# HGRN2 decay-level scores in 64 x 64 blocks on the two halves of the output partitions, in a fused hybrid-decoder step on one core

## Chip, cores, metric

One NeuronCore of a Trainium2 chip. The metric is the device time of one launch in microseconds, lower is better. The kernel before runs in 2715.94 us (median of three runs, 2710.35 to 2718.6).

## What is computed

The reference is one inference step of a two-layer decoder trunk (`D_MODEL` 2048, 512 prompt tokens and 8 single-token samples, all float32). Each layer projects the normalised input to the columns of 16 heads of width 128 (4 HGRN2, 6 mLSTM, 6 retention), runs the recurrences, gates the result and projects it back. The change is in the HGRN2 heads:

```python
b = jnp.cumsum(gc, axis=2)                       # gc: log forget gate, per key channel
diff = b[:, :, :, None, :] - b[:, :, None, :, :]
decay = jnp.exp(jnp.where(mask[:, :, None], diff, -jnp.inf))
a = jnp.einsum('bhtk,bhsk,bhtsk->bhts', qc, kc, decay)
intra = jnp.einsum('bhts,bhsv->bhtv', a, vc)
```

The score of query t and key s is a sum over 128 channels, each with its own decay from s to t, so one matmul of q and k doesn't give it.

## The kernel before

Tokens stand along the free axis: 512 prompt tokens and 8 samples, 520 columns, in two halves of 260 (`HALF`). Every weight tile of 2048 x 128 is multiplied by the normalised input in a split of three products: `quarter` (L501 to L512) issues, for each of 16 row blocks, high weights by high input, high weights by low input and low weights by high input, twice each for the two halves (all of them are recorded as L509). `tile` (L605 to L613) runs a tile as 8 parts of 12 matmuls. Each head has four tiles (for HGRN2: forget gate, query, value, output gate). TensorE (PE) executes in program order. The small matmuls of a head are "hooks" that stand between the parts of later tiles, so that the waits of the recurrence lie beside projection work.

An HGRN2 head works on four chunks of 128 tokens. The score matrix `a` (a view of buffer `t1`: partitions are keys s, four chunks, 128 queries t) is built level by level. Level -1 is the diagonal (key and query of the same token, `k` times `x1`). Level v = 0 to 6 holds the pairs whose tokens lie in one group of 2^(v+1), the key in its first half and the query in its second. For it, the keys are decayed to the end of their half (`kdec(v)`, made by `k_step(v)` on VectorE (DVE) as one multiply and one copy of 256 elements a partition, L1338 and L1339) and the queries from the start of theirs (`q_step(v)`, in place in `qd`, L1344).

`level_scores` (L701 to L722) is the hook. For a level it waits for the queries (`vs["lev"]`), from level 3 on also for its PSUM bank to be free again (`vs["pred"]`), and multiplies, for each of four chunks, 128 keys by 128 queries into partitions 0 to 127 of bank `(lv + 1) % 4` of `mx` (L716 for level -1, L719 for the others). Levels -1 and 0 stand together after part 2 of the head's value tile, levels 1 to 5 after parts 3 to 7, level 6 after part 0 of the output-gate tile (L794 to L796). Then `rows` follows after part 2 (transposes, L515 and L518), `states_u` after part 5 (L733, L737), `outputs` after part 7 (L745, L747, L756) and `back` after part 5 of the next head's first tile.

DVE, in its own program order, makes the key levels 1 to 4 together with the products of decays `fold(m)` (L1355 to L1359), then the level-0 queries (L1362), and then for each level (L1365 to L1378): wait for the score, make the next level's queries, signal them, and take the score out of PSUM. The diagonal is taken by a multiply with the identity, which writes zeros elsewhere (L1372); each other level by a predicated copy of 128 x 512 with the level's mask (L1374). After levels 1, 2 and 3 it makes key levels 5, 6 and 7. `kdec(7)` is used only by `rows` (L671).

Other queues: ScalarE (ACT) takes projections out of PSUM and makes the high part of the weights, GpSimd (POOL) the low part (L480), SP issues the weight loads. Matmuls in which the output has few partitions are placed at partitions 0, 32, 64, 96 in several parts of the kernel: the adaLN projection (L590 and L575, 32 weight columns), the gates (L629, 6 columns), the sample rows (L518, 2 columns, and L756).

Of the kernel before, what the change touches and what calls it, by code (L numbers as in the profile page):

```python
# [126 lines left out]
def program(nc, x_prompt, x_sample, st_hg, st_c, st_n, st_m, st_conv, st_rt, c_prompt, c_sample, g_norm,  # L127
# [3 lines left out]
    with ExitStack() as ctx:  # L131
# [137 lines left out]
        def kdec(m):  # L269

            return k[:, 0:T] if m == 0 else lev[:, m - 1, :]
# [228 lines left out]
        def _(e):  # L500
# [47 lines left out]
            for l in range(DEPTH):  # L548
# [102 lines left out]
                def hooks_of(h):  # L651
# [49 lines left out]
                        def level_scores(vs_range):  # L701

                            def run():
                                for lv in vs_range:
                                    if lv < 0:
                                        e.wait_ge(as_["kk"], n + 1)
                                        e.wait_ge(taken, ht(g, 1))
                                    else:
                                        e.wait_ge(vs["lev"], n * LEVELS + (lv + 1))
                                    if lv >= 3:  # L710
                                        e.wait_ge(vs["pred"], n * (LEVELS + 1) + (lv - 2))
                                    bank = (lv + 1) % 4
                                    for c in range(NC):
                                        cs = slice(c * CH, (c + 1) * CH)
                                        if lv < 0:
                                            last = e.matmul(mx[:, bank, cs], k[:, cs], x1[:, PAD + c * CH:PAD + (c + 1) * CH],  # L716
                                                            start=True, stop=True)
                                        else:
                                            last = e.matmul(mx[:, bank, cs], kdec(lv)[:, cs], qd[:, cs],  # L719
                                                            start=True, stop=True)  # L720
                                    last.then_inc(ps["score"], 1)
                            return run  # L722

# [363 lines left out]
        def _(e):  # L1087
# [53 lines left out]
            for l in range(DEPTH):  # L1141
# [100 lines left out]
                for h in range(NH):  # L1242
# [39 lines left out]
                        if kind == "rt":  # L1282
                            chunk_decay, token_decay = hc[:, HC_CD:HC_CD + NC], hc[:, HC_G:HC_G + NS]
                            e.wait_ge(hc_in[g % 2], 16 * (n // 2 + 1))
                            e.wait_ge(rope_in, 16 * (l + 1))
                            rope(0, q)
                            tt(qd[:], q[:, 0:T], hc[:, HC_IN:HC_IN + T], M)
                            rope(1, k)
                            e.drain().then_inc(vs["qk"], 1)

                            e.wait_ge(ps["score"], scorec(l, kind, i, 1))
                            tt(a, mx[:, 0, :].rearrange("p (c t) -> p c t", c=NC), bc(hc[:, HC_D:HC_D + CH], 1, NC),
                               M)
                            e.drain().then_inc(vs["a"], 1)
                        elif kind == "ml":
                            chunk_decay, token_decay = gcol[:, i, 3, :], gsb[:, i, :]
                            e.wait_ge(ps["bcast"], n + 1)
                            tt(dt[:].rearrange("p (c t) -> p c t", c=NC), mx[:, 0, :].rearrange("p (c t) -> p c t", c=NC),
                               bc(gcol[:, i, 0, :], 2, CH), A_)
                            e.drain()  # L1300
                            tt(dt[:].rearrange("p (c t) -> p c t", c=NC), dt[:].rearrange("p (c t) -> p c t", c=NC),
                               bc(cst[:, C_NEG:C_NEG + 128], 1, NC), A_)
                            e.drain().then_inc(vs["r"], 1)
                            e.wait_ge(taken, ht(g, 0))
                            e.wait_ge(as_["cvc"], n + 1)
                            conv(0, t1, "conv_q")
                            e.wait_ge(as_["lg"], 2 * n + 1)
                            log_sigmoid(t3[:], t1[:], "ls")
                            e.wait_ge(as_["silu"], 2 * n + 1)
                            tt(q[:], t1[:], t3[:], M)  # L1310
                            e.wait_ge(taken, ht(g, 1))
                            conv(1, t2, "conv_k")
                            e.wait_ge(as_["iw"], n + 1)
                            tt(qd[:], q[:, 0:T], iw, M)
                            e.drain().then_inc(vs["qd"], 1)
                            e.wait_ge(as_["lg"], 2 * n + 2)
                            log_sigmoid(t4[:], t2[:], "ls")
                            e.wait_ge(as_["silu"], 2 * n + 2)
                            stt(k[:], t2[:], SCALE, t4[:], M, M)
                            e.drain().then_inc(vs["qk"], 1)  # L1320
                            e.wait_ge(ps["score"], scorec(l, kind, i, 1))
                            tt(t1[:, 0:T], mx[:, 0, :], dt[:], M)
                            e.drain().then_inc(vs["a"], 1)
                        else:
                            chunk_decay, token_decay = sm[:, 16:16 + NC], t3[:, T:TOK]

                            def paired(ap, m):

                                return ap.rearrange("p (n s x) -> p n s x", s=2, x=1 << (m - 1))

                            def folded(m, s):

                                return fold(m - 1)[:, s::2].unsqueeze(2).broadcast_to([P, T >> m, 1 << (m - 1)])

                            def k_step(m):

                                new, old = paired(kdec(m), m), paired(kdec(m - 1), m)
                                tt(new[:, :, 0, :], old[:, :, 0, :], folded(m, 1), M)  # L1338
                                e.tensor_copy(new[:, :, 1, :], old[:, :, 1, :])  # L1339

                            def q_step(m):

                                w = paired(qd[:], m)
                                tt(w[:, :, 1, :], w[:, :, 1, :], folded(m, 0), M)  # L1344

                            e.wait_ge(as_["l1"], n + 1)
                            f = x0[:, PAD:PAD + TOK]
                            stt(t2[:], f, 0.0, t1[:], MIN, S_)
                            e.drain()
                            tt(t4[:], t2[:], f, S_)  # L1350
                            e.drain().then_inc(vs["d1"], 1)
                            e.wait_ge(as_["kk"], n + 1)
                            ts(t3[:], t3[:], lbv[:, 1, i:i + 1], lbv[:, 0, i:i + 1], M, A_)
                            e.drain()
                            for m in range(1, LEVELS + 1):  # L1355
                                tt(fold(m), fold(m - 1)[:, 0::2], fold(m - 1)[:, 1::2], M)
                                if m <= 4:
                                    k_step(m)
                                e.drain()  # L1359

                            e.wait_ge(taken, ht(g, 1))
                            tt(qd[:], x1[:, PAD:PAD + T], t3[:, 0:T], M)  # L1362
                            e.drain().then_inc(vs["lev"], 1)
                            e.sem_inc(vs["qk"], 1)
                            for lv in range(LEVELS):  # L1365
                                e.wait_ge(ps["score"], scorec(l, kind, i, lv + 2))
                                q_step(lv + 1)
                                e.drain().then_inc(vs["lev"] if lv + 1 < LEVELS else vs["kw"], 1)
                                for x in (-1, 0) if lv == 0 else (lv,):
                                    bank = mx[:, (x + 1) % 4, :].rearrange("p (c t) -> p c t", c=NC)  # L1370
                                    if x < 0:
                                        tt(a, bank, bc(ident, 1, NC), M)  # L1372
                                    else:
                                        e.copy_predicated(a, bc(lmask[:, 128 * x:128 * x + 128], 1, NC), bank)  # L1374
                                    e.drain().then_inc(vs["pred"], 1)
                                if 1 <= lv <= 3:
                                    k_step(lv + 4)
                                    e.drain()  # L1378
                            e.sem_inc(vs["a"], 1)


# [176 lines left out]
```

## Time and profile before

| | us |
|---|---|
| median of 3 runs | 2715.94 (2710.35 to 2718.6) |
| the profiled execution | 2717.08 |
| its span, first to last instruction | 2715.3 |
| PE busy with matmuls | 2492.0 (92%) |
| DVE busy | 1142.8 (42%) |
| POOL busy | 932.8 (34%) |
| ACT busy | 795.9 (29%) |

A record is one instruction in the trace. A float32 matmul leaves two MATMUL records and two weight-load records (a transpose leaves one of each), so `level_scores` leaves 8 records of each kind for a level. The ends of matmuls are modelled and include the way through the array, so of a run of matmuls the distance of starts counts, not the duration. In the timeline, a row "x8" with a start and a length merges eight records; their mean distance is the length less the duration of one, divided by seven. The HGRN2 heads of the first layer lie at 264 to 510 us of the span, those of the second at 1527 to 1772 us.

### The profile page before, as it was taken

The page shows a single profiled execution, that of the slowest core. Times are in us where ns is not written, and L with a number is a line of the kernel's source. Part 1 is how long each engine was busy: PE and PEld are TensorE (multiplying, and loading weights), DVE is VectorE, ACT ScalarE, POOL GpSimd, SP SyncE. Part 2 cuts the span into 40 slices and gives each one's busy share as a digit, 9 for nine tenths or more (in the row PEclk, how much of TensorE's full clock was granted, in tenths as well). Part 3 has the DMA queues.
Part 4 walks back from the last instruction along what each step waited for, and adds up shares of the span by engine and source line. Part 5 has one row for each costly group of instructions (what it writes and reads, how often), then busy time and mean ns, then how long its engine had stood idle before and what let it go on. Part 6 is the DMA issues. An engine that isn't in the chain of part 4 may idle for free.

```text
span 2715.3 us, 48497 instructions
## 1 busy us (share of the span) xinstructions
PE 2492.0 (92%) x20592; PEld 2244.4 (83%) x20592; DVE 1142.8 (42%) x2239; ACT 795.9 (29%) x1247; POOL 932.8 (34%) x676
## 2 busy tenths in 40 slices
PE   3776999799999999989998799979999999998996
PEld 2115999699999999987776799969999999998995
DVE  2004555367767433430000755546677534333002
ACT  1004222233433332331112322323333323333113
POOL 0002343233434444462221343414434444446440
PEclk9998999899999999999999899989999999998998
DMA  5995333133334343429987233323333333433421
GB/s 176 319 310 156 90 85 96 49 83 100 96 96 103 103 113 101 108 67 299 294 277 236 70 81 93 80 68 87 94 104 100 103 105 101 110 97 95 116 80 63
DMA packets 473218, 339.70 MB, mean 125 GB/s; under 512 B 17701, under 2 KB 416513, under 8 KB 471681
## 3 DMA queue, kind: packets, MB, share of 16 engines
q1 hardware_dynamic: 473002, 336.61, 43.1%
q8 instruction: 162, 2.65, 0.4%
q14 instruction: 54, 0.44, 0.1%
HBM read 304.72 MB, written 32.04 MB: 124 GB/s over the span
## 4 chain that ended last, share of the span: by engine, by line
PE 76%; DVE 8%; DMA 7%; ACT 3%; DVEq 2%; POOL 2%; issue 1%; SPq 1%; ACTq 0%
PE pj L509 59%; DMA raw<-in_w_ada 4%; PE mx L515 2%; PE mx L544 2%; PE mx L719 2%; DMA raw<-in_w_out 2%; POOL wlo L480 1%; PE pj L590 1%; ACT whi L862 1%; PE mx L575 1%; PE mx L518 1%; DVE t L1095 1%; PE mx L733 1%; PE mx L629 1%; DVEq L1188 1%
## 5 line engine op out<-in xcount | busy, mean ns | idle before, releaser
L480 POOL TENSOR_TENSOR wlo<-raw,whi 128x512 fp32r<-128x512 f32 x640 | 890.3, 1422 | 1710.6 <-ACT whi L862 1710.6
L509 PE MATMUL pj<-hh,whi 128*128 128x260 f32 x5120 | 1067.6, 290 | 61.9 <-POOL wlo L480 33.2
L509 PE MATMUL pj<-hh,wlo 128*128 128x260 f32 x5120 | 1036.7, 284 | 0.0
L509 PE MATMUL pj<-hl,whi 128*128 128x260 f32 x5120 | 1035.6, 284 | 0.0
L509 PEld LDWEIGHTS pj<-hh,whi 128*128 128x128 f32 x5120 | 793.5, 190 | 139.9 <-issue 101.6
L509 PEld LDWEIGHTS pj<-hl,whi 128*128 128x128 f32 x5120 | 795.5, 190 | 0.0
L509 PEld LDWEIGHTS pj<-hh,wlo 128*128 128x128 f32 x5120 | 795.0, 190 | 0.0
L862 ACT ACTIVATE whi<-raw 128x2048 fp32r<-128x2048 f32 x160 | 306.3, 1915 | 314.5 <-DMA raw<-in_w_out 170.7
L1095 DVE SCALAR_TENSOR_TENSOR o<-pj,mod,t 128x260 f32<-128x260 f32 x64 | 28.0, 480 | 397.8 <-PE pj L509 397.8
L862 ACT ACTIVATE xv<-pj 128x260 f32<-128x260 f32 x192 | 66.2, 384 | 433.7 <-PE pj L509 433.3
L590 PE MATMUL pj<-raw,sct 128*32 128x512 f32 x384 | 102.5, 668 | 45.9 <-DMA raw<-in_w_ada 45.4
L862 ACT ACTIVATE t<-t 128x520 f32<-128x520 f32 (+1 forms) x132 | 84.3, 639 | 186.1 <-DVEq L1279 133.3
L590 PEld LDWEIGHTS pj<-raw,sct 128*32 128x32 f32 x384 | 14.5, 113 | 124.5 <-DMA raw<-in_w_ada 122.9
L1095 DVE SCALAR_TENSOR_TENSOR t<-xv,prm,t 128x512 f32<-128x512 f32 x96 | 103.6, 1099 | 5.5
L862 ACT ACTIVATE z<-pj 128x260 f32<-128x260 f32 x64 | 21.3, 385 | 271.4 <-PE pj L509 271.4
L862 ACT ACTIVATE t<-pj 64x260 f32<-64x260 f32 (+1 forms) x108 | 43.8, 405 | 152.2 <-PE pj L590 151.1
L1089 DVE TENSOR_TENSOR mod<-mx,bia 128x432 f32<-128x432 f32 x2 | 1.2, 607 | 174.8 <-PE mx L561 173.7
L1089 DVE TENSOR_TENSOR xv<-xv,lev 128x520 f32<-128x520 f32 x24 | 16.8, 701 | 136.0 <-ACT t L862 135.5
L862 ACT ACTIVATE zw<-zw 128x520 f32<-128x520 f32 x96 | 61.3, 638 | 24.2 <-DVEq L1252 19.9
L1409 DVE COPY st<-mx 128x128 f32<-128x128 f32 (+1 forms) x32 | 9.4, 293 | 131.2 <-PE mx L737 131.2
L1089 DVE TENSOR_TENSOR t<-mx,hc 128x512 f32<-128x512 f32 x12 | 8.3, 693 | 130.1 <-PE mx L697 130.1
L515 PE MATMUL mx<-cst,xv 128*128 128x128 f32 (+1 forms) x376 | 54.2, 275 | 3.9 <-DVEq L1484 3.7
(231 smaller groups left out, 2229.3 us busy)
## 6 DMA issues: line engine op xcount, KB each, us to landing
raw<-in_w_in SPq DMA_DIRECT2D x256, 512.0 KB, 5.3
raw<-in_w_ada SPq DMA_DIRECT2D x96, 512.0 KB, 5.4
raw<-in_w_out SPq DMA_DIRECT2D x64, 512.0 KB, 6.2
lev<-in_w_ada SPq DMA_DIRECT2D x58, 512.0 KB, 4.9
xv<-in_w_ada SPq DMA_DIRECT2D x38, 512.0 KB, 5.5
out<-ss SPq DMA_DIRECT2D x32, 512.0 KB
y_kept<-o SPq DMA_DIRECT2D x2, 4160.0 KB, 12.8
t<-y_kept SPq DMA_DIRECT2D x32, 260.0 KB, 4.5
```

What stands on the lines that cost most here:

```text
L480: last = e.tensor_tensor(wlo[:, par, cs], w[:, cs], whi[:, par, cs].bitcast(F32), ALU.subtract)
L509: last = e.matmul(pj[:, 2 * par + b, 0:HALF], w[:, par, kb * P:(kb + 1) * P], x[:, kb, b * HALF:(b + 1) * HALF], start=(kb == 0 and m == 0 ...
L515: return e.transpose(out, src, cst[0:n, C_ID:C_ID + n])
L518: return e.matmul(out, src, cst[0:n, C_ID:C_ID + n], start=True, stop=True)
L544: last = e.matmul(mx[:, b, 0:HALF], ones, (t1, t2)[kb % 2][:, b * HALF:(b + 1) * HALF], start=(kb == 0), stop=(kb == KB - 1))
L575: last = e.matmul(mx[r:r + 32, n % 2, :], sct[:, kb, :], ada_slot(piece)[:, j, :], start=(kb < 4), stop=(kb >= KB - 4))
L590: last = e.matmul(pj[r:r + 32, n % 2, :], sct[:, kb, :], raw[:, s % RAW, j * ADA_N:(j + 1) * ADA_N], start=(kb < 4), stop=(kb >= KB - 4))
L629: last = e.matmul(mx[32 * j:32 * j + H_ML, 0, 0:HALF], w, x[:, kb, (j // 2) * HALF:(j // 2 + 1) * HALF].bitcast(F32), start=(kb == 0 and m ...
L719: last = e.matmul(mx[:, bank, cs], kdec(lv)[:, cs], qd[:, cs], start=True, stop=True)
L733: last = e.matmul(mx[:, c, 0:w], kt[:, c, :], vt[:, c, 0:w], start=True, stop=True)
L862: return e.activation(out, in_, func, **kw)
L1095: return e.scalar_tensor_tensor(out=out, in0=a_, scalar=s, in1=b_, op0=op0, op1=op1)
```

## The change

In the scores, the chunk's 128 keys and 128 queries are cut into blocks of 64. Levels -1 to 5 have pairs only inside the two diagonal blocks, so two matmuls of 64 weight columns by 64 moving columns are issued for a chunk: block b goes to output partitions 64b to 64b+63, and the bank then holds 256 columns instead of 512. Level 6 has pairs only between the first 64 keys and the second 64 queries: one matmul a chunk, into partitions 0 to 63.

```diff
 for c in range(NC):
-    cs = slice(c * CH, (c + 1) * CH)
-    if lv < 0:
-        last = e.matmul(mx[:, bank, cs], k[:, cs], x1[:, PAD + c * CH:PAD + (c + 1) * CH],
-                        start=True, stop=True)
-    else:
-        last = e.matmul(mx[:, bank, cs], kdec(lv)[:, cs], qd[:, cs],
-                        start=True, stop=True)
+    for b in range(1 if lv + 1 == LEVELS else 2):
+        s0 = c * CH + 64 * b
+        t0_ = s0 + 64 if lv + 1 == LEVELS else s0
+        key = k if lv < 0 else kdec(lv)
+        query = x1[:, PAD + t0_:PAD + t0_ + 64] if lv < 0 else qd[:, t0_:t0_ + 64]
+        last = e.matmul(mx[64 * b:64 * b + 64, bank, 64 * c:64 * c + 64],
+                        key[:, s0:s0 + 64], query, start=True, stop=True)
 last.then_inc(ps["score"], 1)
```

On DVE the lower left quarter of `a`, which no selection writes any more, is zeroed once per head; key levels 5 to 7 are made before the levels; each selection becomes two instructions, one for each half of the partitions, of 64 partitions by 256 elements; level 6 is a plain copy.

```diff
+e.memset(a[64:128, :, 0:64], 0.0)
 e.wait_ge(taken, ht(g, 1))
 tt(qd[:], x1[:, PAD:PAD + T], t3[:, 0:T], M)
 e.drain().then_inc(vs["lev"], 1)
 e.sem_inc(vs["qk"], 1)
+for m in range(5, LEVELS + 1):
+    k_step(m)
+    e.drain()
 for lv in range(LEVELS):
     e.wait_ge(ps["score"], scorec(l, kind, i, lv + 2))
     q_step(lv + 1)
     e.drain().then_inc(vs["lev"] if lv + 1 < LEVELS else vs["kw"], 1)
     for x in (-1, 0) if lv == 0 else (lv,):
-        bank = mx[:, (x + 1) % 4, :].rearrange("p (c t) -> p c t", c=NC)
-        if x < 0:
-            tt(a, bank, bc(ident, 1, NC), M)
-        else:
-            e.copy_predicated(a, bc(lmask[:, 128 * x:128 * x + 128], 1, NC), bank)
+        bank = mx[:, (x + 1) % 4, 0:256].rearrange("p (c t) -> p c t", c=NC)
+        for b in range(1 if x + 1 == LEVELS else 2):
+            r = slice(64 * b, 64 * b + 64)
+            if x < 0:
+                tt(a[r, :, r], bank[r], bc(ident[r, r], 1, NC), M)
+            elif x + 1 == LEVELS:
+                e.tensor_copy(a[0:64, :, 64:128], bank[r])
+            else:
+                mk = lmask[r, 128 * x + 64 * b:128 * x + 64 * b + 64]
+                e.copy_predicated(a[r, :, r], bc(mk, 1, NC), bank[r])
         e.drain().then_inc(vs["pred"], 1)
-    if 1 <= lv <= 3:
-        k_step(lv + 4)
-        e.drain()
```

## Rows read from the trace of the kernel before

**Rows 1.** The page: busy time of the engines, chain that ended last.

```profile
PE 2492.0 (92%) x20592; PEld 2244.4 (83%) x20592; DVE 1142.8 (42%) x2239; ACT 795.9 (29%) x1247; POOL 932.8 (34%) x676
...
PE 76%; DVE 8%; DMA 7%; ACT 3%; DVEq 2%; POOL 2%; issue 1%; SPq 1%; ACTq 0%
```

**Rows 2.** 264 to 510 us: PE, PEld, DVE, ACT, POOL busy; clock, DMA. PE's waits.

```profile
264.00:510.00 246.00, 242.61 (x2110) 234.93 (x2114) 129.06 (x302) 70.45 (x106) 92.40 (x64) 1.00 0.33 86
...
PE mx L515 <- DVEq L1484: 2.9, 4, 0.8
```

**Rows 3.** The chain in order of time, first head: start, length, what.

```profile
282.04 0.89 PE mx L716 x8
...
283.82 1.44 PE pj L509 x12
285.26 0.89 PE mx L719 x8
```

**Rows 4.** PE timeline, single levels and the projection matmuls behind them.

```profile
282.77 1.06 PE L719 MATMUL mx<-qd,xv 128*128 128x128 f32 x8
...
283.90 0.40 PE L509 MATMUL pj<-hl,whi 128*128 128x260 f32 x2
...
74.90 1.06 PE L561 MATMUL mx<-cst,t 128*128 128x9 f32 x8
```

**Rows 5.** Weight loads by shape: busy us, mean ns.

```profile
L719 PEld LDWEIGHTS mx<-qd,lev 128*128 128x128 f32 x384 | 46.9, 191 | 0.0
...
L575 PEld LDWEIGHTS mx<-lev,sct 128*32 128x32 f32 x232 | 6.0, 108 | 5.9 <-DMA lev<-in_w_ada 2.0
```

**Rows 6.** Timeline of matmuls and weight loads placed at several output partitions.

```profile
73.92 0.62 PE L590 MATMUL pj<-raw,sct 128*32 128x512 f32 x2 [0.94 <-DMA raw<-in_w_ada]
...
73.92 1.05 PE L590 MATMUL pj<-raw,sct 128*32 128x512 f32 x4 [0.94 <-DMA raw<-in_w_ada]
...
73.92 0.14 PEld L590 LDWEIGHTS pj<-raw,sct 128*32 128x32 f32 x4 [1.85 <-DMA raw<-in_w_ada]
...
509.84 0.62 PE L629 MATMUL mx<-hh,gw 128*6 128x260 f32 x8
510.28 0.62 PE L629 MATMUL mx<-hl,gw 128*6 128x260 f32 x8
```

**Rows 7.** Timeline around the sample rows and around an 11-column transpose.

```profile
301.26 0.27 PE L515 MATMUL mx<-cst,lev 128*128 128x128 f32 x1
301.46 0.29 PE L518 MATMUL mx<-cst,xv 128*2 128x128 f32 x4
...
301.79 0.51 PE L518 MATMUL mx<-cst,xv 128*2 128x128 f32 x12
...
302.57 0.28 PE L509 MATMUL pj<-hl,whi 128*128 128x260 f32 x1
...
560.47 0.38 PE L515 MATMUL mx<-cst,xv 128*11 128x128 f32 x2
560.60 0.49 PE L509 MATMUL pj<-hh,whi 128*128 128x260 f32 x2
```

**Rows 8.** DVE timeline of the first head's levels; a zero fill (busy, mean ns).

```profile
279.90 0.69 DVE L1089 TENSOR_TENSOR qd<-xv,t 128x512 f32<-128x512 f32 x1
283.86 0.61 DVE L1089 TENSOR_TENSOR qd<-qd,t 128x256 f32<-128x256 f32 x1 [3.27 <-PE mx L719]
...
285.40 0.74 DVE L1374 COPY_PREDICATED t<-lmask,mx 128x512 f32<-128x512 uint8 x1
286.26 0.43 DVE L1089 TENSOR_TENSOR qd<-qd,dt 128x256 f32<-128x256 f32 x1
...
287.66 0.43 DVE L1089 TENSOR_TENSOR lev<-lev,dt 128x256 f32<-128x256 f32 x1
288.00 0.29 DVE L1339 COPY lev<-lev 128x256 f32<-128x256 f32 x1
...
L1118 DVE MEMSET nr<- 128x256 f32 x1 | 0.3, 272 | 0.0
```

## The prediction

> **What bounds the kernel now.** I read the page first: PE is busy for 92% of the span and makes 76% of the chain that ended last, while DVE is busy for 42% [rows 1]. The change touches only the eight HGRN2 heads (four in each layer), so the stretch counts, not the average. Over the first layer's four heads (246 us), PE is busy for 242.61 us and DVE for 129.06, at a granted clock of 1.00, the upper level of 2.4 GHz. The one repeated wait of PE there is 2.9 us in four, before the transposes of `back`, and none stands before a level's score [rows 2]. The chain in order of time runs through PE there: a level takes 0.89 us, the 12 matmul records of the projection part behind it take 1.44 us, then comes the next level [rows 3]. So PE's program is the bound in these stretches. What a hook gains or loses on PE reaches the end, and what DVE does costs nothing while it is ready before PE's next level.
>
> **What a level costs PE now.** Eight records, (1.06 - 0.27) / 7 = 0.11 us apart [rows 4], make the 0.89 us. The adaLN sums of L561 have the same weight load of 128 columns and only 9 moving columns, and stand (1.06 - 0.26) / 7 = 0.11 us apart too [rows 4]: the load of 128 columns takes that time by itself, and the stream of 128 columns about the same, beside it.
>
> **What 64 by 64 records cost.** The load shrinks with the weight columns: a mean of 191 ns for 128 and 108 for 32 is 0.86 ns a column [rows 5], or 0.055 us for 64. The stream: the gates start four records of 260 columns, one for each quarter of the output partitions, every 0.22 us (eight in 510.28 - 509.84 = 0.44 us) [rows 6], 0.85 ns a column, so 0.054 us for 64. With 3 to 5 ns between records, as 0.111 is above 128 times 0.85, I take 0.058 us.
>
> Do the two halves run together? Nothing here is placed in two halves, but much in quarters. In the adaLN projection two matmuls of different quarters both start at 73.92, and all four are done after 1.05 us, two times 0.43 and the way through the array; the four weight loads lie within 0.14 us, before the first two streams end [rows 6]. So for parts of different output partitions both loads and streams overlap, and I take the same for halves. A level of 16 records is then eight pairs, 8 x 0.058 = 0.46 us. Level 6 has eight records all in the lower half, which take turns, and costs 8 x 0.058 = 0.46 us as well.
>
> **What the change adds on PE: two switches a hook.** Where a matmul of all output partitions is followed by one placed in a part, the distance isn't 0.11 but 301.46 - 301.26 = 0.20 us, so going in costs 0.09. The last of the sample rows starts at 301.79 + 0.51 - 0.27 = 302.03; the second pair of projection matmuls behind it starts at 302.57, 0.54 later [rows 7]. Behind a level of before that distance is 283.90 - (282.77 + 1.06 - 0.27) = 0.34 [rows 4]. Going out costs 0.20. The first load of 64 columns lies bare behind the switch, 0.055. Together 0.345, say 0.35 us for each hook, paid seven times a head.
>
> **The sum on PE**
> - Hook with levels -1 and 0: before 16 x 0.111 = 1.78 us. After 2 x 0.46 + 0.35 = 1.27. Gain 0.51.
> - Five hooks with levels 1 to 5: before 0.89, after 0.46 + 0.35 = 0.81. Gain 0.08 each, 0.40.
> - Hook with level 6: the same, 0.08.
> - A head gains 0.99 us, eight heads 7.9 us.
>
> The bounds of the two terms that no row shows for halves: the distance of pairs lies between 0.055 (half of 0.11) and 0.065 us (if a few ns more go to each record), the switch between 0.29 (the bare load hidden) and 0.40. The best corner gives 0.61 + 6 x 0.16 = 1.57 us a head, 12.6 in all; the worst 0.34 + 6 x -0.03 = 0.16 us a head, 1.3 in all.
>
> **DVE, beside PE.** Added before the level-0 queries: a zero fill of 256 elements, at most 0.27 us. Moved ahead: three key steps, each of a multiply (287.66) and a copy that ends at 288.29, with its drain 0.74 us, so 2.2. Together 2.5 us go into the 3.27 us in which DVE waited for the first score [rows 8]. That score now comes 0.7 us earlier (0.93 + 0.145 for the way in, against 1.78), so the idle time left is about 0.1 us; and the level-1 scores stand 1.44 us later in PE's program, against 0.61 for the queries. Each selection in two instructions costs a little more than in one: 256 elements take 0.43 against 0.69 for 512, and the second can start 0.34 us after the first (as 288.00 follows 287.66), so 0.77 against 0.69, and alike for the predicated copies. Two levels' selections take some 0.16 more, and the level-2 queries, signalled at 286.70 before [rows 8] with PE coming for them at about 287.3 (level 1 of rows 3 and 0.89 + 1.44, less 0.16 by which the chain counts later than the timeline, less a load of 0.11), are signalled at about 286.3 with PE coming at 287.3 - 0.51 - 0.08 = 286.7. All later levels are rid of a key step of 0.74 and the cadence of PE's levels (2.24 us) is longer than DVE's work for one (about 1.5). So DVE costs nothing, as long as halves of 64 partitions cost by their elements a partition. If that cover of 0.4 us goes, PE waits for level 2. The step is moved past no DMA and no other queue; `rows` gets `kdec(7)` earlier than it needs.
>
> **Rivals**
> - **The halves take turns.** Then 16 records cost 16 x 0.058 = 0.93 us: levels 1 to 5 lose 0.93 + 0.35 - 0.89 = 0.39 each, the double hook 1.86 + 0.35 - 1.78 = 0.43, level 6 gains 0.08. A head loses 2.3 us, eight lose 18.4: 2734 us. It decides once less than 0.7 of the overlap is had (all of it is worth 7 x 0.46 = 3.2 us a head, of which 2.3 are needed to be even). For it: no row shows halves. Against it: all placed matmuls of rows 6 and 7 overlap.
> - **Loads don't run beside a stream.** Then a pair takes 0.055 + 0.054, 0.11 us, a level 0.89 as before, and each hook the 0.35 of its switches more than now: 7 x 0.35 x 8 = 19.6 us, 2736. Against it: the four loads in 0.14 us, beside streams of 0.43 [rows 6]. The Trainium skill, "TensorE: Matmul & The Clock Gate", section "The mechanism" of the part on packing small matmuls, says this: a weight load overlaps matmuls in flight only when its row group differs, and here all row groups are the same. The trace disagrees with it.
> - **DVE comes late.** Were a selection of 64 partitions as long as one of 128 (0.69 and 0.74 each), the level-2 queries would come 2 x 0.55 later than I have them, about 0.7 us after PE wants them, and the later ones would catch up. Eight times 0.7 gives back 5.6: 2713.6 us.
> - **No separate placement.** The 11-column transposes are followed by projection 0.13 us after their start, without a switch [rows 7]. If the 64-column matmuls were treated so, 16 records in turn would cost 0.93 without switches: 7 x 0.04 lost, 0.43 gained at level 6, 0.15 a head: 2715 us. Against it: the upper half must go to partitions 64 to 127.
>
> **How the numbers follow.** The profiled execution took 2717.08 us (span 2715.3), 1.1 above the median of 2715.94. I take the 7.9 from the median: 2708 us. The same step from the profiled execution gives 2709.2. Measurements of this kernel tell a difference of about 0.3%, 8.1 us, from none, and the forecast lies at that edge. Chances: forecast 0.66 (2703 to 2715), DVE late 0.12, no placement 0.06, halves in turn 0.12, loads in series 0.04. Of the forecast's 0.66 I give 0.40 to over 0.3% faster and 0.26 to within; DVE late and no placement fall within 0.3%; the last two are slower. That makes 0.40, 0.44, 0.16. The range is 2702 to 2720: it takes in the corners and leaves out the two slower cases and a tail below.
>
> **What would show it.** Per level 16 score records of 64 columns in pairs some 5 to 10 ns apart, pairs 0.058 us apart; in the chain 0.8 us from part to part instead of 0.89, and the double hook 1.27 instead of 1.78; the distance of two heads' `rows` shorter by 1.0 us. Right on DVE: no wait of PE for `qd`, and DVE's first wait for a score under 0.5 us. The prediction is wrong if records of the upper half start only after those of the lower, if the step from the last score to the second pair of projection matmuls is longer than 0.54 less 0.05, or if PE waits for DVE at level 1 or 2.

## The result, and the profile after

The changed kernel runs in 2734.92 us (median of four runs), the kernel before in 2715.04 in the same comparison: a ratio of 1.0071, 95% interval 1.0056 to 1.0086. It is slower by 20 us, where 8 us faster was forecast. The profiled execution has a span of 2733.7 us against 2715.3.

The page shows that PE's work didn't grow: its busy time is what it was [rows 1], while its share of the chain fell from 76% to 70%.

```profile
PE 2493.2 (91%) x21040; PEld 2233.1 (82%) x21040; DVE 1184.9 (43%) x2303; ACT 796.4 (29%) x1247; POOL 937.6 (34%) x676
...
PE 70%; DVE 11%; DMA 6%; ACT 5%; DVEq 3%; issue 2%; POOL 1%; ACTq 1%; SPq 0%
```

The view of PE's waits over the whole span has a row that no view of before had. L1372 is the drain behind the level queries, the instruction with which DVE waits for its own multiply to end before it signals, so PE stands 24.1 us before scores and waits for queries, up to 3.2 us at a time:

```profile
PE mx L719 <- DVEq L1372: 24.1, 10, 3.2
```

The PE timeline of the first head shows both halves of the story (start, length, group; in brackets the idle time before it). Levels -1 and 0 are exactly what was forecast; the wait stands before level 1:

```profile
280.01 0.41 PE L509 MATMUL pj<-hh,wlo 128*128 128x260 f32 x2
280.35 0.69 PE L719 MATMUL mx<-xv 128*64 128x64 f32 x16
280.86 0.64 PE L719 MATMUL mx<-qd,xv 128*64 128x64 f32 x16
281.43 0.51 PE L509 MATMUL pj<-hh,whi 128*128 128x260 f32 x2
281.77 0.41 PE L509 MATMUL pj<-hl,whi 128*128 128x260 f32 x2
...
286.00 0.69 PE L719 MATMUL mx<-qd,lev 128*64 128x64 f32 x16 [2.87 <-DVEq L1372]
```

The weight loads of the first 16 records lie beside their matmuls:

```profile
280.35 0.55 PEld L719 LDWEIGHTS mx<-xv 128*64 128x64 f32 x16
```

The chain from the wait, in order of time, shows that the wait costs more than its own length:

```profile
286.00 0.69 PE mx L719 x16
286.69 2.51 PE pj L509 x12
289.20 1.05 PE mx L719 x16
290.25 1.76 PE pj L509 x12
292.01 0.61 PE mx L719 x16
292.63 1.63 PE pj L509 x12
```

The same part of 12 records takes 2.51 us behind the wait and 1.63 later (the switches included), the level 1.05 instead of 0.61. The windows view of the two stretches (PE, PEld, DVE, ACT, POOL busy, then the granted clock) gives the reason: the granted clock is 0.62 behind the wait and 1.00 after it, part of the stretch at the lower of the two levels, 1.2 GHz.

```profile
286.00:290.50 4.50, 4.50 (x45) 4.08 (x46) 3.24 (x8) 0.00 (x0) 0.00 (x0) 0.62 0.84 225
290.50:300.00 9.50, 9.50 (x110) 8.69 (x110) 5.70 (x13) 2.47 (x3) 0.91 (x1) 1.00 0.01 2
```

The last two columns, the share of the DMA engines and GB/s, show a burst of transfers in the same stretch. It isn't the cause: behind the wait of the second head, also of 2.9 us, the DMA share is as high, the clock stays at 1.00, and the parts take 1.62 us as usual:

```profile
350.10:354.60 4.50, 4.25 (x55) 3.90 (x56) 3.87 (x9) 0.00 (x0) 0.00 (x0) 1.00 0.81 221
```

So the clock falls behind most of these waits, not behind all: behind six of the eight in this execution, by the granted clock of the 4.5 us after each (0.62 to 0.65, else 1.00).

Why the queries are late is in DVE's timeline of the same head, with POOL's row under it:

```profile
278.61 0.69 DVE L1089 TENSOR_TENSOR qd<-xv,t 128x512 f32<-128x512 f32 x1
279.51 1.22 DVE L1089 TENSOR_TENSOR lev<-lev,dt 128x256 f32<-128x256 f32 x1 [0.21 <-issue]
280.65 1.36 DVE L1339 COPY lev<-lev 128x256 f32<-128x256 f32 x1
282.09 1.36 DVE L1089 TENSOR_TENSOR lev<-lev,dt 128x256 f32<-128x256 f32 x1
283.37 1.35 DVE L1339 COPY lev<-lev 128x256 f32<-128x256 f32 x1
284.79 0.43 DVE L1089 TENSOR_TENSOR lev<-lev,dt 128x256 f32<-128x256 f32 x1
285.13 0.28 DVE L1339 COPY lev<-lev 128x256 f32<-128x256 f32 x1
285.49 0.42 DVE L1089 TENSOR_TENSOR qd<-qd,t 128x256 f32<-128x256 f32 x1
...
278.67 5.90 POOL L480 TENSOR_TENSOR wlo<-raw,whi 128x512 fp32r<-128x512 f32 x4 [5.57 <-ACT whi L862]
```

The key steps are the instructions of [rows 8], moved to the time from 279.5 on. There POOL works at the low part of a weight tile, from 278.67 to 284.57. Four of the six take 1.22 to 1.36 us instead of 0.43 and 0.29; the pair behind POOL's end takes its old time. The three steps last 5.9 us, not 2.2, and the level-1 queries are signalled at 285.9, where PE wanted them at about 283.1. Both layers' heads do the same.

Where the time went can be measured by stage: from the first level score of a layer's first head to the first matmul of the gates (L629), a stretch with four heads in it, 227.96 and 226.87 us before, 239.41 and 239.81 after. Both layers together give 454.8 and 479.2 us, so 24.4 us more. The spans differ by 18.4; the missing 6 lie mostly in layer one's output stage and the start of layer two, with 5.2 of them between the gates of layer one and the first score of layer two. The change doesn't touch that stretch, and in the runs below it varies between 1028 and 1037 us, so the stage sums are the sharper measure for all of them.

### The profile page after: what moved, and what is told of

Same layout as the page of the kernel before. It is cut to its first block, busy times and chain, and to the rows that moved or that the text cites. A ratio compares the mean times of both kernels' runs of the same rounds, so it can differ in the third digit from the quotient of the medians.

```text
span 2733.7 us, 49457 instructions
## 1 busy us (share of the span) xinstructions
PE 2493.2 (91%) x21040; PEld 2233.1 (82%) x21040; DVE 1184.9 (43%) x2303; ACT 796.4 (29%) x1247; POOL 937.6 (34%) x676
## 4 chain that ended last, share of the span: by engine, by line
PE 70%; DVE 11%; DMA 6%; ACT 5%; DVEq 3%; issue 2%; POOL 1%; ACTq 1%; SPq 0%
PE pj L509 54%; DMA raw<-in_w_ada 4%; PE mx L515 2%; ACT whi L862 2%; PE mx L544 2%; DVE lev L1089 1%; PE mx L575 1%; DVE t L1095 1%; POOL wlo L480 1%; PE pj L590 1%; ACT t L862 1%; PE mx L719 1%; PE mx L518 1%; PE mx L733 1%; PE mx L629 1%
```

## The experiments

Theory A: the PE saving is as forecast, and the loss comes from the key steps ahead of the levels, because there they run beside POOL. Theory B: the blocks or the selections in halves make PE late. All ratios are to the kernel before on the same chip, with 95% intervals. "Stage" is the sum defined above, "waits" are PE's at the level scores.

| run | ratio | stage, us | waits, us |
|---|---|---|---|
| before | | 454.8 | none |
| the change | 1.0071 (1.0056 to 1.0086) | 479.2 | 24.1 in 10 |
| e1 keys back | 0.9955 (0.9941 to 0.9969) | 445.8 | none |
| e2 before, keys ahead | 1.0085 (1.0065 to 1.0106) | 480.8 | 16.1 in 8 |
| e3 POOL light | 0.9946 (0.9925 to 0.9968) | 445.8 | none |
| e4 keys spread | 0.9948 (0.9927 to 0.9969) | 445.8 | none |
| e5 halves in turn | 1.0025 (1.0010 to 1.0039) | 463.3 | none |
| e6 level 6 in pairs | 0.9953 (0.9926 to 0.9979) | 444.3 | none |
| e7 two steps ahead | 1.0057 (1.0040 to 1.0073) | 470.3 | 19.2 in 13 |
| e8 one step ahead | 0.9981 (0.9972 to 0.9990) | 453.4 | 6.4 in 16 |
| e9 POOL cut in 8 | 1.0072 (1.0045 to 1.0098) | 486.4 | 21.1 in 8 |
| e10 before, POOL light | 1.0008 (0.9992 to 1.0025) | 454.8 | none |
| e11 as e6, more rounds | 0.9956 (0.9942 to 0.9970) | 444.3 | none |
| e12 e6 and POOL cut in 8 | 0.9937 (0.9923 to 0.9951) | 442.7 | none |

### Undo the move: e1 and e4

```diff
-for m in range(5, LEVELS + 1):
-    k_step(m)
-    e.drain()
 for lv in range(LEVELS):
     ...
+    if 1 <= lv <= 3:          # e4: if lv in (1, 3, 5): k_step(5 + lv // 2)
+        k_step(lv + 4)
+        e.drain()
```

> The change, but key levels 5 to 7 made behind levels 1 to 3 again, as before. Theory A (the key steps ahead of the levels run beside GpSimd's low parts, are stretched from some 2.2 us to 5.9 us by them, and make PE wait 2.9 us for the level-1 queries in each head): PE's waits for L719 fall from 24.1 us to under 2 us, no clock window at half level inside the heads, and the PE saving stands: 2707 to 2710 us. DVE's work for levels 1 to 3 is then 0.55 + 1.0 + 0.85 = 2.4 us against PE's 2.24, so up to 0.1 us of wait a head at level 4 or 5. Theory B (selections in halves or the blocks themselves make PE late): stays above 2725 us.

> The change, but key level 5 made behind level 1, 6 behind 3, 7 behind 5. Theory A: DVE's work for two levels is 1.55 + 2.4 = 3.95 us against PE's 4.48, so PE never waits for L719: 2707 to 2709 us, as e1 or up to 1 us below it. Theory B: above 2725 us.

Both came out as theory A has them, a little faster than their bands (by 1.0 and 0.3 us): 2705.96 and 2706.73 us, no wait at the scores, and a stage sum of 445.8 us, 9.0 less than before. The heads follow each other every 59.63 us in e4, against 60.61 in layer two of before: 0.98 us a head, for 0.99 forecast. Theory B falls. The PE timeline of e4 has the cadence of the forecast, 284.32 - 282.08 = 2.24 us a level:

```profile
282.08 0.69 PE L719 MATMUL mx<-qd,lev 128*64 128x64 f32 x16
282.69 0.51 PE L509 MATMUL pj<-hh,whi 128*128 128x260 f32 x2
283.04 0.40 PE L509 MATMUL pj<-hl,whi 128*128 128x260 f32 x2
...
284.32 0.69 PE L719 MATMUL mx<-qd,lev 128*64 128x64 f32 x16
```

### The move alone: e2

```diff
 e.sem_inc(vs["qk"], 1)
+for m in range(5, LEVELS + 1):
+    k_step(m)
+    e.drain()
 ...
-    if 1 <= lv <= 3:
-        k_step(lv + 4)
-        e.drain()
```

> The kernel before, with only one part of the change: key levels 5 to 7 ahead of the levels. Theory A: DVE is at them from 280.8 to about 286.5 us in the first head, the level-1 queries come near 287 where PE wants them at 285.0: about 2 us of wait in each of eight heads, 16 us, and some falls of the clock of 0.9 us each: 2731 to 2737 us. Theory B, or if the steps fit into DVE's 3.27 us of waiting: 2714 to 2718 us.

The waits are as theory A has them, 2.0 us in each of eight heads, and the steps are stretched alike (1.22, 1.36, 1.34 and 1.36 us for the first four). The time is 2742.44 us, 5 above the expected band: the stage grew by 26 us, of which 16.1 are waits and 10 what came behind them, so I had that part too low.

```profile
PE mx L719 <- DVEq L1371: 16.1, 8, 2.0
```

### Take POOL away: e3, and its control e10

```diff
-    low(i * 4 + (l * TILES + j), j % 2)
+    low(i * 4 + (l * TILES + j), j % 2, 16 if i < H_HG and j == 3 else None)
```

`low` then makes 16 columns in each of its four instructions for these tiles and leaves out the other 496, so these weights lack most of their low part.

> The change as it is, but GpSimd makes only 16 of 512 columns of each quarter of the low part for the HGRN2 heads' output-gate tiles (the rest of that low part is left out), so that it is idle while DVE makes key levels 5 to 7. Theory A: each key multiply takes 0.42 and each copy 0.29 us again, DVE's first queries come about 283.2 us, PE's waits for L719 vanish: 2706 to 2710 us. Rival C (GpSimd has no part in it, the steps are slow there or simply too much): the steps stay at 1.2 to 1.36 us and the time at 2730 us or more.

> Control for the run with a light GpSimd: the kernel before, with the same part of the low weights left out (16 of 512 columns in the HGRN2 heads' output-gate tiles). Nothing waited for them, so 2712 to 2717 us, at most 3 us from the kernel before; if it gains 8 us or more, the light run of the change didn't show what theory A says.

This settles the cause. With the change's order kept, the timeline of DVE and POOL's row read:

```profile
277.80 0.42 DVE L1089 TENSOR_TENSOR lev<-lev,dt 128x256 f32<-128x256 f32 x1 [0.21 <-issue]
278.14 0.31 DVE L1339 COPY lev<-lev 128x256 f32<-128x256 f32 x1
278.52 0.42 DVE L1089 TENSOR_TENSOR lev<-lev,dt 128x256 f32<-128x256 f32 x1
...
276.95 1.58 POOL L480 TENSOR_TENSOR wlo<-raw,whi 128x16 fp32r<-128x16 f32 x4 [5.57 <-ACT whi L862]
```

The steps are back at 0.42 and 0.29 us, the three of them end at 279.9, 2.1 us after they began, and no wait is left: 2702.91 us, some 3 us below the expected band, with a stage sum of 445.8 as in e1. POOL isn't wholly idle there: its four short instructions run until 278.53, and the multiply and the copy beside them take 0.42 and 0.31 us. So it isn't POOL's being busy by itself that holds DVE, but the length of its instructions, which e9 tries again. The same lighter POOL gave the kernel before nothing (2713.79 us, ratio 1.0008, stage 454.8), so it isn't POOL's work as such that costs, only DVE's key steps beside it. Rival C falls.

### The dose: e7 and e8

```diff
-for m in range(5, LEVELS + 1):
+for m in range(5, 7):         # e8: range(5, 6)
     k_step(m)
     e.drain()
 ...
+    if lv == 3:               # e8: levels 6 and 7 behind 2 and 4
+        k_step(7)
+        e.drain()
```

> The change with key levels 5 and 6 ahead and 7 behind level 3. Theory A (the wait grows by what DVE does ahead while GpSimd works): in the change the third key step already ran behind GpSimd's end at its own 0.7 us, so the level-1 queries come 0.7 us earlier and PE waits 2.2 us a head instead of 2.9; with fewer falls of the clock: 2720 to 2730 us. If any step ahead of the levels makes PE wait by its own length alone (0.7 us), then 2708 to 2713 us.

> The change with key level 5 alone ahead, 6 behind level 2, 7 behind level 4. Theory A: the one step, stretched to 2.6 us, ends near 282.1 us in the first head's time of the change, about when the first score is there; the level-1 queries, themselves beside GpSimd, come near 283.2, as PE does: 0 to 0.4 us of wait a head, 2705 to 2711 us.

The waits come down from 24.1 to 19.2 and 6.4 us, as theory A orders them. In e7 they are 2.4 us a head, where 2.2 was expected, and it took 2731.51 us, 1.5 above its band. In e8 they are 0.8 us a head, twice the most expected: the level-1 wait is 0.42 to 0.44 us in seven heads and 1.57 in one, and a second of 0.23 us or a little more stands before level 2. Its time, 2709.36 us, lies in its band. The level-1 wait comes from the query multiply itself, which now starts beside POOL; the DVE timeline of e8:

```profile
283.20 1.22 DVE L1089 TENSOR_TENSOR lev<-lev,dt 128x256 f32<-128x256 f32 x1 [0.21 <-issue]
284.35 1.36 DVE L1339 COPY lev<-lev 128x256 f32<-128x256 f32 x1
285.78 1.35 DVE L1089 TENSOR_TENSOR qd<-qd,t 128x256 f32<-128x256 f32 x1
```

### What the stretch is made of: e9

```diff
-LOW_CUT = 4
+LOW_CUT = 8
```

> The change as it is, with GpSimd's low part cut into 8 instructions of 256 columns a tile instead of 4 of 512, the same work. Theory F (a DVE instruction with SBUF operands on both sides gets its turn only when a GpSimd instruction ends: in the change's trace four key instructions in a row take 1.22 to 1.36 us and end 0.15 to 0.3 us behind the ends of four GpSimd instructions of 1.3 to 1.8 us): the key instructions take about 0.7 us, the six of them some 4 us instead of 5.9, PE waits 1 to 1.7 us a head instead of 2.9: 2714 to 2724 us. Rival G (the two engines share bandwidth, so what counts is how long they overlap): the waits stay near 24 us, 2730 us or more.

The price missed, the mechanism held. The DVE timeline of e9's second head:

```profile
351.80 1.21 DVE L1089 TENSOR_TENSOR qd<-xv,t 128x512 f32<-128x512 f32 x1
353.22 0.66 DVE L1089 TENSOR_TENSOR lev<-lev,dt 128x256 f32<-128x256 f32 x1 [0.21 <-issue]
353.81 0.81 DVE L1339 COPY lev<-lev 128x256 f32<-128x256 f32 x1
354.69 0.80 DVE L1089 TENSOR_TENSOR lev<-lev,dt 128x256 f32<-128x256 f32 x1
355.41 0.82 DVE L1339 COPY lev<-lev 128x256 f32<-128x256 f32 x1
...
357.90 0.79 DVE L1089 TENSOR_TENSOR qd<-qd,t 128x256 f32<-128x256 f32 x1
...
351.72 6.69 POOL L480 TENSOR_TENSOR wlo<-raw,whi 128x256 fp32r<-128x256 f32 x8 [4.98 <-ACT whi L862]
```

Each DVE instruction now takes 0.66 to 0.82 us, about one of POOL's shorter instructions (a mean of 0.83 us in this run). Multiply and copy cost the same, though alone they take 0.42 and 0.29. So neither bandwidth nor length of overlap sets the time; the two engines take turns, one instruction each. Eight POOL instructions catch eight DVE instructions where four had caught four: the 0.69 us multiply of `qd` took 1.21, the six key instructions and the level-1 query multiply followed. Up to the end of that multiply the change needs 7.3 us from the start of `qd`, e9 6.9. The wait fell only from 24.1 / 8 = 3.0 to 2.6 us a head, and the ratio not at all (1.0072). DVE leaves such a stretch only when POOL does, if it has instructions enough to be caught by all of it: the last caught one ends at 284.72 in the change, where POOL ends at 284.57, and at 358.69 in e9, where POOL ends at 358.41.

The stage sum even grew, by 7.2 us, though the waits fell by 3.0: in this execution (2745.89 us, the slowest of the four) the clock fell behind all eight waits and stayed low for longer. Levels 1 and 2 and the parts behind them take 7.3 us in the second head, by the chain, where 4.5 is usual. The windows behind that head's wait:

```profile
358.80:363.30 4.50, 4.50 (x38) 4.16 (x40) 3.04 (x7) 0.00 (x0) 0.00 (x0) 0.50 0.88 230
363.30:367.80 4.50, 4.50 (x49) 4.17 (x46) 2.23 (x6) 0.00 (x0) 0.00 (x0) 0.80 0.01 4
```

Against it stands a shorter end of the kernel: from the first matmul of the gates of layer two to the last instruction it is 938.3 us instead of the change's 944.1.

### Do the halves overlap whatever the order: e5

```diff
-for c in range(NC):
-    for b in range(1 if lv + 1 == LEVELS else 2):
+for b in range(1 if lv + 1 == LEVELS else 2):
+    for c in range(NC):
```

> As e4, but PE's program has all four lower blocks of a level first and then the four upper ones. If PE starts records in program order (theory D), the halves overlap only at the seam: a level of 16 records takes some 0.87 us instead of 0.46, seven levels a head, eight heads: +23 us against e4, 2727 to 2732 us; this is also what the rival 'halves take turns' would have cost. If PE's queue reaches the upper half past the waiting lower ones (theory E; within a pair the two passes already start as lower, upper, lower, upper though the program has them lower, lower, upper, upper), then as e4: 2704 to 2709 us.

Between both: 2721.62 us, and 61.81 us a head against 59.63, 0.31 us for each of the seven levels where 0.41 would be no overlap but at the seam. In PE's timeline of e5 the first record of level 0 (`qd,xv`, by the program the lower half) starts at 290.23, when level -1 (`xv`) has three records (by the program of the upper half) left to start, and then the two alternate; a level by itself is the last row:

```profile
289.82 0.63 PE L719 MATMUL mx<-xv 128*64 128x64 f32 x11
290.23 0.27 PE L719 MATMUL mx<-qd,xv 128*64 128x64 f32 x1
290.28 0.22 PE L719 MATMUL mx<-xv 128*64 128x64 f32 x1
290.34 0.22 PE L719 MATMUL mx<-qd,xv 128*64 128x64 f32 x1
...
292.75 0.97 PE L719 MATMUL mx<-qd,lev 128*64 128x64 f32 x16
```

PE reaches past waiting records of one half to those of the other, but only a few deep (three in these rows). That PE executes in program order, as the section on the kernel before has it, therefore doesn't hold between the two halves. A level takes 0.97 us (to the modelled end) in blocks by halves and 0.69 alternating, so the alternation in the program is worth 15 us of this kernel.

### A version that beats both: e6, e11 and e12

Level 6 has eight records in one half. Its chunks 2 and 3 can go to the upper half, with DVE bringing them back:

```diff
-last = e.matmul(mx[64 * b:64 * b + 64, bank, 64 * c:64 * c + 64],
+up = c // 2 if lv + 1 == LEVELS else b
+last = e.matmul(mx[64 * up:64 * up + 64, bank, 64 * c:64 * c + 64],
 ...
-e.tensor_copy(a[0:64, :, 64:128], bank[r])
+e.tensor_copy(a[0:64, 0:2, 64:128], bank[0:64, 0:2])
+e.tensor_copy(a[0:64, 2:4, 64:128], bank[64:128, 2:4])
```

(with level 6's chunks in the order 0, 2, 1, 3, and the key steps as in e4).

> As e4, but level 6's blocks of chunks 2 and 3 go to the upper half of the partitions, so that its eight records run as four pairs too; DVE copies them back in two instructions of 64 x 128. Theory A: level 6 takes 0.23 us instead of 0.46: 1.8 us less over eight heads, 2703 to 2706 us; in the trace the hook's eight records start within 0.18 us. If DVE's two copies made PE late at the row transposes, there would be a wait at L515 behind DVE; none is expected, PE comes there 2.9 us later.

> The best version once more with more rounds (key steps spread behind levels 1, 3 and 5, level 6 in pairs): ratio to the kernel before 0.995 to 0.997, 2703 to 2708 us.

> The same with GpSimd's low part in 8 instructions. PE waits for nothing in the heads already, so no gain there: within 2 us of the run before it, unless GpSimd's longer total (a fixed cost for each instruction) shows where PE waits for it in the output stage, some 30 us in all now: then 2 to 5 us more.

The eight records of level 6 take 0.45 us to the modelled end in e11's PE timeline, not the 0.68 of e4:

```profile
297.32 0.45 PE L720 MATMUL mx<-qd,lev 128*64 128x64 f32 x8
```

That is 0.22 us a head (59.41 against 59.63), a stage sum of 444.3 us, and 2702.48 and 2702.10 us in two comparisons. The intervals of the ratios of e4, e6 and e11 overlap, so the gain over e4 rests on the stage sums and the head distances, not on the times. e12 adds the cut of POOL's work in 8 and is the fastest, 2697.74 us, ratio 0.9937, where I expected nothing or a small loss. Its stage sum is 442.7, 1.6 less than e11, with 59.23 us a head; I didn't trace which instructions bring the 0.18 us a head. The larger part of its gain lies outside the heads: from the first matmul of the gates of layer two to the end it takes 939.1 us, e11 943.7, as e9 did against the change. What makes that part shorter isn't traced either.

## Why the prediction was wrong, step by step

- **What bounds the kernel**: right. The stage sums in the table follow PE's own time, its waits and the clock behind them; e12's last 1.6 us are untraced.
- **Pairs overlap, 0.46 us a level**: right. In the change, pairs stand 0.058 us apart ((0.64 - 0.22) / 7 = 0.06 by the row at 280.86, for eight pairs). The rival of halves that take turns gives nearly the measured time, 2734 against 2734.92, and is wrong all the same: the two records of a pair start within 0.01 us, and with the key steps put back the same PE program gains 9 us. A time that fits is no proof of its mechanism.
- **Loads that don't run beside a stream**: refuted by the same rows: a pair every 0.058 us leaves no room for a load of 0.055 us in front of a stream of 0.054. The rule of the Trainium skill, "TensorE: Matmul & The Clock Gate", section "The mechanism", that a weight load overlaps matmuls in flight only when the row group differs, doesn't hold for the two column halves here.
- **Two switches, 0.35 us a hook**: right. From the last pair (280.86 + 0.64 - 0.22 = 281.28) to the second pair of projection matmuls at 281.77 it is 0.49 us, the 0.54 forecast from the sample rows less 0.05 of a shorter stream. The way in is 280.35 against the last projection matmul near 280.14, 0.21.
- **The sum on PE, 7.9 us**: right in mechanism and size once nothing stands in its way. The stage gained 9.0 us in e1 and e4, of which 8 x 0.98 = 7.8 is the forecast; the rest is in the main small waits of PE on DVE elsewhere in the heads: 4.7 us in both layers before, 2.9 of them in layer one [rows 2], and 3.6 in e4.
- **DVE, beside PE: the step that failed.** I put "2.5 us" into the "3.27 us in which DVE waited for the first score". The 2.5 came from key steps at 287.66, when POOL was idle; the gap they moved into is the one in which POOL works. Priced there, they take 5.9 us. [Rows 8] had the sign: the level-1 query multiply took 0.61 us and the next one, as large, 0.43. I read the gap for its length and not for who else was busy in it. What came is the last of the signs that the prediction names for its being wrong, a wait of PE for DVE at level 1. The rival "DVE comes late" had the right victim and a wrong cause (selections by halves, whose pairs cost 0.86 and 0.90 us, only some 0.1 more than forecast) and a price of 5.6 us for 24.1.
- **What a wait costs**: missing from the forecast altogether. The change's stage is 33.4 us above e4's and the waits make 24.1 of it. Most of the other 9.3 is the fall of the granted clock behind six of them: in the chain above, the two parts and the level between them take 5.32 us instead of 3.87, 1.45 more. Six times 1.45 is 8.7 us. Two of the six distances of heads in the change are 62.88 and 63.24 us, the other four 64.03 to 64.08; the two begin with the heads behind whose wait the clock stayed at 1.00, and they hold a second wait of 0.25 us that the four don't have. Why the clock fell behind some waits of the same length and not behind others stays open.

## To carry to other kernels

Before moving work into an engine's idle time, look at what the other engines do in that time and price the moved instructions by rows taken beside the same neighbour: in this kernel DVE's multiplies of two SBUF tensors and its copies within SBUF take turns with POOL's instructions, and DVE's reads of PSUM don't. Small matmuls in two halves of the output partitions run in pairs if the program alternates the halves, at 0.3 us or more of switches for each group, so such groups should be few and large. And a stall of PE of 2.9 us cost half as much again through the clock in six of eight cases.

## What the runs showed of the hardware

DVE beside POOL. The row of one form in the kernel before, both of its inputs in SBUF, has a median of 420 ns and a maximum of 1518 (min/median/max ns):

```profile
L1089 DVE TENSOR_TENSOR lev<-sr,cst x44: 406/420/1518, 302.9 to 2446.2; 98x256 f32<-98x256 f32 x44
```

The selections, which read scores from PSUM, are not caught. In the kernel before, the multiply with the identity at 284.59 lies whole beside POOL's last instruction (284.15 to 285.62) and takes the 0.69 us it takes alone; the predicated copies take 733 to 755 ns in all 56. Nor is every instruction that reads SBUF caught: the statistics of a head's output (BATCH_NORM_STATS2), with one input, take 274 to 297 ns in all 128, 80 of which lie beside POOL's work.

```profile
284.59 0.69 DVE L1089 TENSOR_TENSOR t<-mx,cst 128x512 f32<-128x512 f32 x1
...
L1460 DVE BATCH_NORM_STATS2 bst<-xv x128: 274/277/297, 318.5 to 2466.2; 128x6 f32<-128x128 f32 x128
```

POOL waits too: its four instructions of the first head take 5.90 us in the change and 5.33 before, where fewer DVE instructions meet them:

```profile
280.29 5.33 POOL L480 TENSOR_TENSOR wlo<-raw,whi 128x512 fp32r<-128x512 f32 x4 [5.55 <-ACT whi L862]
```

The Trainium skill, "GPSIMD Engine Reference", section "Specifications", names GpSimd's SBUF interfaces as shared with VectorE, with contention for DVE instructions in a two-port mode or with two SBUF inputs. The trace agrees in kind for the multiplies, and for the statistics, which have one input. The copies are caught as well; whether they run in a two-port mode, no run shows. The trace adds the size: each such DVE instruction takes about as long as the POOL instruction it meets, 1.36 us for 512 columns (the change) and 0.8 for 256 (e9).

PE places. The two records of a pair start together, and a switch between matmuls of all output partitions and placed ones costs 0.09 us in and 0.20 out. The Trainium skill, "TensorEngine Tiling (Array Packing)", section "Key Properties", says that a change of tiling mode drains the engine. Whether the 0.29 us are that drain no row shows; they are a third of a level of before (0.89).
